# Differential attention's stage: two conv tiles on TensorE from shifted copies, and the rotary swap by ScalarE

## The reference

```
q, k, v, u = split(h @ w_in)                       # 512, 512, 512, 1024 columns
q, k = partial_rope(q), partial_rope(k)            # first 16 of each 64 dims: t1*cos - t2*sin, t2*cos + t1*sin
a = softmax(q1 k1) v - lam * softmax(q2 k2) v      # 4 heads, two 64-wide halves each, causal
a = rmsnorm(a)
c = u[:, :512] * sigmoid(u[:, 512:])
c = causal_depthwise_conv(c, w[31, 512]) + b       # 31 taps per channel
c = silu(layernorm(c))
y = concat(a, c) @ w_out
```

## Time and profile before

| | |
|---|---|
| median of three runs | 2302.03 us (2301.68 to 2302.09) |
| span of the profiled execution, first to last instruction | 2299.9 us |
| that execution's own time outside the span | not printed; median less span is 2.1 us |
| mean granted TensorE clock | 0.999 |
| TensorE busy | 2275.5 us, 99% |
| VectorE, ScalarE, GpSimd busy | 1272.2, 654.6, 1570.5 us |
| DMA | 200.17 MB, mean 87 GB/s |

### The profile page before, as it was taken

The page is one execution under the profiler, slowest core; times in us unless marked ns, Lnnn a source line. Parts: engine busy times, 40 slices in busy tenths (PEclk is TensorE's granted clock), DMA queues, the critical chain, the costliest instruction groups (busy, mean ns, idle before and its releaser), DMA issues.

```text
span 2299.9 us, 27958 instructions
## 1 busy us (share of the span) xinstructions
PE 2275.5 (99%) x10600; PEld 1863.7 (81%) x10600; DVE 1272.2 (55%) x1828; ACT 654.6 (28%) x1213; POOL 1570.5 (68%) x1532
## 2 busy tenths in 40 slices
PE   8999999999999999999999999999999999999998
PEld 6888888888887788888788888888668788888887
DVE  7774745335345777166545364459875345626354
ACT  3443432101013455154311011142344233202113
POOL 8666568777776455545597777678327938878784
PEclk9999999999999999999999999999999999999999
DMA  4222232333332111212243333333113413333332
GB/s 169 82 74 86 70 92 92 105 96 97 96 97 92 51 39 49 74 34 60 73 129 100 97 114 101 93 97 105 56 37 92 124 56 92 96 98 96 99 94 76
DMA packets 112727, 200.17 MB, mean 87 GB/s; under 512 B 12497, under 2 KB 21201, under 8 KB 112593
## 3 DMA queue, kind: packets, MB, share of 16 engines
q1 hardware_dynamic: 109424, 194.72, 27.2%
q10 hardware_dynamic: 3168, 3.67, 0.5%
HBM read 196.24 MB, written 2.10 MB: 86 GB/s over the span
## 4 chain that ended last, share of the span: by engine, by line
PE 93%; DVE 4%; POOL 1%; ACT 1%; issue 0%; DMA 0%; SPq 0%; DVEq 0%; POOLq 0%; ACTq 0%
PE bank L479 27%; PE bank L481 27%; PE bank L480 27%; DVE bank L1996 1%; DVE h L1988 1%; PE bank L949 1%; PE bank L1075 1%; PE bank L528 1%; POOL wL L2857 1%; PE bank L918 1%; PE bank L919 1%; PE bank L920 1%; PE bank L598 1%; DVE aL L1996 1%; PE bank L663 1%; PE bank L926 1%
## 5 line engine op out<-in xcount | busy, mean ns | idle before, releaser
L2857 POOL TENSOR_TENSOR wL<-raw,wH 128x512 fp32r<-128x512 f32 (+2 forms) x732 | 1006.2, 1375 | 61.1
L2855 POOL TENSOR_SCALAR wH<-raw 128x512 fp32r<-128x512 f32 (+2 forms) x732 | 528.6, 722 | 553.5 <-PE bank L481 477.9
L479 PE MATMUL bank<-aH,wH 128*128 128x512 f32 (+2 forms) x1392 | 548.1, 394 | 8.6 <-DVE aL L1996 7.6
L481 PE MATMUL bank<-aH,wL 128*128 128x512 f32 (+2 forms) x1392 | 539.7, 388 | 0.0
L480 PE MATMUL bank<-aL,wH 128*128 128x512 f32 (+2 forms) x1392 | 539.6, 388 | 0.0
L479 PE MATMUL bank<-uH,wH 128*128 128x512 f32 (+1 forms) x1010 | 384.1, 380 | 0.0
L480 PE MATMUL bank<-uL,wH 128*128 128x512 f32 (+1 forms) x1010 | 382.4, 379 | 0.0
L481 PE MATMUL bank<-uH,wL 128*128 128x512 f32 (+1 forms) x1010 | 382.4, 379 | 0.0
L479 PEld LDWEIGHTS bank<-aH,wH 128*128 128x128 f32 (+1 forms) x1392 | 261.8, 188 | 64.7 <-POOL wL L2857 6.6
L480 PEld LDWEIGHTS bank<-aL,wH 128*128 128x128 f32 (+1 forms) x1392 | 261.8, 188 | 55.5 <-issue 3.2
L481 PEld LDWEIGHTS bank<-aH,wL 128*128 128x128 f32 (+1 forms) x1392 | 261.7, 188 | 54.3
(11 more groups left out here) (330 smaller groups left out, 3194.1 us busy)
## 6 DMA issues: line engine op xcount, KB each, us to landing
raw<-in_ws SPq DMA_DIRECT2D x698, 256.0 KB, 2.5
raw<-in_ws SPq DMA_DIRECT2D x24, 192.0 KB, 2.3
h<-in_xT SPq DMA_DIRECT2D x8, 256.0 KB, 6.0
E<-in_memT ACTq DMA_DIRECT2D x16, 128.0 KB, 2.6
raw<-in_ws SPq DMA_DIRECT2D x10, 128.0 KB, 2.1
tmp<-in_pT ACTq DMA_DIRECT2D x4, 256.0 KB, 2.9
out<-c_F SPq DMA_DIRECT2D x2, 512.0 KB, 2.9
out<-c_F SPq DMA_DIRECT2D x2, 384.0 KB, 2.9
```

What stands on the lines that cost most here:

```text
L479: P.e.matmul(o, lH, rH, start=start, stop=False, skip_group_check=skip)
L481: return P.e.matmul(o, lL, rH, start=False, stop=stop, skip_group_check=skip)
L2855: G.e.tensor_scalar(H, x, 1.0, 0.0, MUL, ADD).then_inc(*G.did("wH", n))
L2857: G.e.tensor_tensor(L, x, H.bitcast(F32), SUB).then_inc(*G.did("w", n))
```

## The change

Tiles 2 and 3 of the convolution are TensorE's, tiles 0 and 1 VectorE's. For each of the two, and for each group i of 32 channels, ScalarE's queue issues four DMAs that copy the 32 rows of the gated input into `d_xr[t][i]`, each time one column further, so that one 128-row operand holds four taps of 32 channels. GpSimd builds the weights `d_tw[t]` (128x1024) from a 32-wide identity and the taps (`spread`), among the gate's weight pieces. `conv_rounds` then issues 8 rounds of four matmuls per tile, each 128 rows by 32 columns of weights at its own column position, into 32 partitions of the tile's bank. They go in groups of 16 matmuls. The columns of q and k are ordered anew in the weight pieces (`rotary_spans`), so that the rotary swap exchanges whole groups of 32 partitions; ScalarE does it with four copies of 32 partitions from the bank, and the permutation matmul goes. VectorE's multiply by cos still waits for ScalarE's `rt`. The memory keys move ahead: tile 4 into head 0's part, 5 and 6 into head 1's, 7 into `d_scores(3)`. `xvalues(0)` is opened (its two banks taken) before head 3's transposes, with half of its steps there.

```diff
 def plan():
+            if layer and 4 <= o < 4 + len(BY_PE):
+                spread[len(out)] = o - 4
             tile8("w_ple_gate", layer, 128 * o)
...
+        if h == 3:
+            tile8("w_ckv_2", 0, 128 * 5)
+        add("w_in_2", 0, k8, rotary_spans(128 * h))
+        add("w_in_2", 0, k8, rotary_spans(512 + 128 * h))
+        if h > 1:
+            tile8("w_ckv_2", 0, 128 * (2 * h))
+    tile8("w_ckv_2", 0, 128 * 7)
...
-BY_PE = 3
+BY_PE, BY_DVE = (2, 3), (0, 1)
...
+            def conv_rounds(t, r0, r1):
+                if r0 == 0:
+                    taps[t] = take("ctap", t)
+                    P.wait_ge(G, "tw", t)
+                    P.wait_ge(xr_in[t], 3, 3)
+                for r in range(r0, r1):
+                    for i in range(4):
+                        c = slice(32 * i, 32 * i + 32)
+                        j = P.e.matmul(taps[t].ap[c, :], d_tw[t][:, 128 * r + 32 * i:128 * r + 32 * i + 32],
+                                       d_xr[t][i][:, 4 * r:4 * r + 512], start=r == 0, stop=r == 7, skip_group_check=True,
+                                       tile_position=(0, 32 * i))
+                if r1 == 8:
+                    j.then_inc(*P.did("ctap", t))
+                    give(taps[t], V, "conv", BY_PE[t])
...
             rotary_in(0)
             rotary_in(1)
-            rotate(0)
-            rotate(1)
-            conv_taps(0, 8)
-            d_scores(0, {1: lambda: conv_taps(8, 12), 2: lambda: rotary_in(2)})
+            conv_rounds(0, 0, 4)
+            d_scores(0, {1: lambda: conv_rounds(0, 4, 8), 2: lambda: rotary_in(2)})
             rotary_in(3)
-            rotate(2)
-            rotate(3)
-            conv_taps(12, 16)
+            conv_rounds(1, 0, 4)
             for hd in range(2):
                 d_turned(hd)
-                d_scores(hd + 1, {1: lambda: conv_taps(16 + 8 * hd, 20 + 8 * hd), 2: lambda: rotary_in(2 * hd + 4)})
+                d_scores(hd + 1, {1: lambda: memory_key(4, 1) if hd else conv_rounds(1, 4, 8), 2: lambda: rotary_in(2 * hd + 4)})
                 rotary_in(2 * hd + 5)
-                rotate(2 * hd + 4)
                 d_values(hd)
-                rotate(2 * hd + 5, second=True)
-                conv_taps(20 + 8 * hd, 23 + 8 * hd)
+                memory_key(4 + 2 * hd, 0)
                 stat_end("dn", hd, tiles=1, tail=False)
-                if hd == 0:
-                    conv_taps(23, 24)
             d_turned(2)
...
-            d_scores(3, {1: lambda: memory_keys(4)})
-            memory_keys(6)
+            d_scores(3, {1: lambda: memory_key(6, 1)})
+            d_values(2)
             b = take("stat", "ln")
...
-            d_values(2)
+            values_opened = xvalues_open(0)
+            xvalues_steps(values_opened, range(4))
             d_turned(3)
-            stat_end("dn", 2, tiles=1, tail=False)
-            xvalues(0)
+            stat_end("dn", 2, tiles=1, tail=False, nth=1)
+            xvalues_steps(values_opened, range(4, 8))
             d_values(3)
...
+            def replicate(t):
+                A.wait_ge(V, "glu", BY_PE[t])
+                A.wait_ge(V, "pad")
+                for i in range(4):
+                    for j in range(4):
+                        A.e.dma_start(d_xr[t][i][32 * j:32 * j + 32, :],
+                                      d_cp[32 * i:32 * i + 32, BY_PE[t], j + 1:j + 541]).then_inc(*xr_in[t].did(i, j))
...
-                do(tmp[j % 2][:, :], bk("rt", j)[:, :], ACT.Copy).then_inc(*A.did("rt", j))
+                for q in range(4):
+                    i = do(tmp[j % 2][quarter_rows(q ^ 1), :], bk("rt", j)[quarter_rows(q), :], ACT.Copy)
+                i.then_inc(*A.did("rt", j))
...
-                V.wait_ge(P, "rts", j)
-                stt(t, bk("rts", j)[:, :], s, Sn[:, :], MUL, MUL).then_inc(*V.did("rts", j))
+                V.wait_ge(A, "rt", j)
+                stt(t, t, s, Sn[:, :], MUL, MUL).then_inc(*V.did("rts", j))
...
+            def convolved(t):
+                V.wait_ge(P, "ctap", t)
+                ts(d_acc[:, BY_PE[t], :], bk("ctap", t)[:, :], vv("cv_dw_b_2", BY_PE[t]), None, ADD, None).then_inc(
+                    *V.did("conv", BY_PE[t]))
...
+            def spread(t):
+                G.wait_ge(P, "down done", 1, 3)
+                G.wait_ge(cs_in)
+                G.wait_ge(vs_in)
+                G.e.tensor_tensor(d_tw[t].rearrange("p (g c) -> p g c", c=32), cc("eye32").unsqueeze(1).to_broadcast([128, 32, 32]),
+                                  vv("cv_tap", 32 * t, 32 * t + 32).unsqueeze(2).to_broadcast([128, 32, 32]), MUL).then_inc(
+                    *G.did("tw", t))
```

More of the change, by code:

```diff
@@ L35, in pieces, with rotary_spans @@
     return [(ks[i:i + n], spans) for i in range(0, len(ks), n)]
+def rotary_spans(c0):
+    return tuple((c0 + 64 * i + c, n) for i in range(2) for c, n in ((0, 8), (16, 24), (8, 8), (40, 24)))
 def plan():
-    out, behind = [], {}
+    out, behind, spread = [], {}, {}
     k8 = tuple(range(8))
@@ L172, in plan @@
         down("w_down_2", 0, ks, True)
-    return out, behind, divided
+    return out, behind, divided, spread
 VECS = [
@@ L446, in pe, with take @@
             at = 0
-            def take(*event, second=False):
-                b = banks.pop(1 if second else 0)
+            def take(*event, nth=0):
+                b = banks.pop(nth)
                 if b.freed:
@@ L1034, in rotary_in @@
             def rotary_in(j):
[L1035 to L1039, removed]
-                P.e.matmul(b.ap[:, :], cc("perm_d"), tmp[j % 2][:, :], start=True, stop=True).then_inc(*P.did("rts", j))
-                give(b, V, "rts", j)
+                linear(("rt", j), (V, "rL", j), "w_in_2", 0, 0, aH, aL, n1_ready,
+                       spans=rotary_spans((512 if j % 2 else 0) + 128 * (j // 2)))
             def d_scores(hd, between={}):
@@ L1066, in pe @@
             taps = {}
-            def conv_taps(k0, k1):
-                if k0 == 0:
-                    taps["bank"] = take("ctap")
-                    P.wait_ge(V, "glu", BY_PE)
-                for k in range(k0, k1):
-                    P.wait_ge(A, "dg", k)
-                    P.e.matmul(taps["bank"].ap[:, :], d_dg[k % 8], d_cp[:, BY_PE, 2 + k:514 + k], start=k == 0, stop=k == 30,
-                               skip_group_check=True).then_inc(*P.did("ctap", k))
-                if k1 == 31:
-                    P.also("ctap")
-                    give(taps["bank"], V, "conv", BY_PE)
+            def conv_rounds(t, r0, r1):
[12 more added lines that the diff above has]
+                    give(taps[t], V, "conv", BY_PE[t])
             def d_turned(hd):
                 for kt in range(4):
-                    b = take("dT", hd, kt, second=hd == 2 and kt == 3)
+                    b = take("dT", hd, kt, nth=1 if hd == 2 and kt == 3 else 0)
                     for n in range(kt, 4):
@@ L1814, in convolved @@
                 do(d_acc[:, i, :], bk_acc(i), ACT.Copy).then_inc(*A.did("conv", i))
-            diagonals(0, 8)
+            for t in range(len(BY_PE)):
+                replicate(t)
             convolved(0)
@@ L1832, in act @@
             convolved(1)
-            diagonals(8, 12)
-            d_scores(0, {2: lambda: (diagonals(12, 16), rotary_in(2))})
+            d_scores(0, {2: lambda: rotary_in(2)})
             rotary_in(3)
@@ L1842, in act @@
                     d_turned(0)
-                d_scores(hd + 1, {2: lambda: (convolved(2) if hd else None, diagonals(20 + 8 * hd, 28 + 8 * hd), rotary_in(2 * hd + 4))})
+                d_scores(hd + 1, {2: lambda: rotary_in(2 * hd + 4)})
+                if hd:
+                    memory_keys(4)
                 rotary_in(2 * hd + 5)
@@ L2514, in taps @@
             def taps():
-                for i in range(3):
+                for i in BY_DVE:
                     y = bk_acc(i)
```

124 lines of the change are left out of this document (76 added, 48 removed), and 2 rows, old and new, of the table VECS.

## The result

The changed kernel takes **2319.96 us** (median of four runs, 2319.86 to 2321.05); the kernel before took 2301.86 us beside it (four runs, 2301.55 to 2302.09). The ratio is 1.0082, with an interval of 1.0070 to 1.0093: 18.1 us slower. The direction was forecast, the size was not: 2309.5 us, with a range that ended at 2314.

What follows compares the result with a forecast made beforehand. TensorE, 99% busy, was taken to bound the kernel through its issued work and waits. Terms -33.5 + 27.5 + 1.2 + 7.9 + 2.0 + 2.4 = +7.5 us on 2302.0 gave 2309.5 us, own range 2304 to 2314.

Steps and rivals of the forecast that it cites:

- At nothing: Changes priced at no time: fewer VectorE taps, ScalarE's diagonals gone, its 32 DMA issues, the copies' traffic, reordered weight columns.
- The convolution, two streams: 27.5 us.: TensorE's 64 column-tile matmuls: never more than two stream at once, one new each 0.43 us, adding 27.5 us.
- rival (a): Convolution on TensorE: four matmuls stream at once, 13.7 us instead of 27.5, kernel at 2299.1 us; chance 0.25.
- The bank of `xkL 6`: 7.4 us.: At the opening of `xvalues`: TensorE idles 7.4 us until VectorE frees the second bank (7.9 with the earlier `stat ln` wait).
- The clock: 2.0 us.: After the 7.4 us idle at `xvalues`: TensorE runs at half rate for a while, costing 2.0 us (bounds 0 and 3).
- The rotary chain, 5.5 us, is covered: From `rotary_in(1)` to k's low part: about 5.5 us, covered by 6.9 us of convolution; with four streams TensorE waits 2.1.
- Piece 486: 2.4 us late.: GpSimd's weight pieces: building two tap weights takes 5.2 us and makes piece 486 2.4 us late (bounds 0 and 4).
- Banks and heads, +1.2 us: Heads 0 to 2: TensorE's waits for banks, low parts and transposes total 3.3 us against 2.1 before, so +1.2.

Runs made afterwards that it cites:

- before_copies: The kernel before the change, with only the 32 copy issues added on ScalarE's queue at the change's place: 2314.43 us against 2301.25 (1.0058).
- copies_later: The changed kernel with ScalarE's 32 copy issues put behind `convolved(0)` instead of ahead of it: 2307.91 us (1.0029).
- copies_sync: The changed kernel with the 32 copies issued by SyncE between weight loads, none by ScalarE: 2306.82 us (1.0024).
- tile_by_tile: `both` with seven rounds of tile 0 ahead of head 0's scores, issued column tile by column tile instead of round by round: 2315.62 us (1.0062).
- spread_late: `both` with seven rounds of tile 0 ahead of head 0's scores, and GpSimd's tap weights built before pieces 505 and 507: 2294.76 us (0.9971).
- both: The changed kernel with SyncE issuing the 32 copies and `xvalues_open` skipping the bank of `xkL 6`: 2301.04 us against 2301.52 (0.9996).

## Why the prediction was wrong

- **The step that failed** is the sentence under "At nothing": ScalarE's "32 DMA issues come while it has no other work". At that place they cost 12 to 13 us (`before_copies` +13.2, `copies_later` -12.0, `copies_sync` -13.1). ScalarE had one small copy behind them, `convolved(0)`, and VectorE stood still until it came. I asked whether ScalarE was busy and when the data would land, and not who waits for the instruction behind the issues; nor did I price an issue: 0.64 us, 20.5 us for 32.
- **"The convolution, two streams: 27.5 us."** It is 13.7, rival (a)'s price. My argument was that starts keep program order and each fp32 matmul has two records. `tile_by_tile` shows that starts keep order only within a column tile; the rows of the changed kernel show four at one time.
- **"The bank of `xkL 6`: 7.4 us."** Right: 7.2 in the trace. Taking it away gave 6.0 us.
- **"The clock: 2.0 us."** Right in kind, too small: one fall was forecast, three came, about 7.5 us; the one behind `x_kL` cost 1.6. I had tied it to an idle time of 7 us; it came behind 2.0 us of wait and behind three waits under 0.8 us too. My reading of the start was weaker than I wrote: its rows give the pitch of 0.44 us, but a granted clock of 1.00 beside it. Behind the wait for `x_kL` the same matmuls start 0.43 us apart at a granted 0.50.
- **"The rotary chain, 5.5 us, is covered"**, and with four streams TensorE waits 2.1 us: with the issues away it waits 2.9. The four copies take 2.39 us where I had 2.2.
- **"Piece 486: 2.4 us late."** 1.0 in the trace; the mechanism was right (`spread_late`). What was off is the price of a tap weight: 1.92 us each, not 2.6, so 3.8 us for both instead of 5.2; with that the working gives the 1.0.
- **Banks and heads, +1.2 us**: measured +5.0. All waits of this part but those of 15.7, 7.2 and 1.0 us make 7.1 us, in place of the 2.1 of before. I take it that with four streams TensorE comes earlier everywhere; no run isolates this.

With four streams and the issues priced, the sum would have been 2309.5 - 13.8 + 3.4 + 13 = 2312. By the account above, the other 8 us are the clock (5.5 more than forecast), waits (1.0) and the 1.6 that are not placed; this is rough, since the 13 hold some of the clock already. **That the direction came out right is luck**: a term 13.8 us too high and one of 13 us left out nearly cancel. Without the error on the issues the right price of the column tiles gives rival (a)'s 2299.1, a faster kernel. (The prediction states two ranges, from 2304 and from 2294; both end at 2314.) Rival (a), "what the change is for", was right about the array and wrong about the time: the gain of 19.8 us on TensorE went into waits and the clock.

## What to carry to other kernels

A DMA issue is an instruction of the engine that issues it: count it at its own price, and look at what stands behind it in that program and who waits for that, before asking when the data lands. When TensorE gets less work between two dependencies, move what is left of it ahead of the wait; the rounds moved ahead here were worth more than their length (5.2 us of cover gave 8.7), because the clock stayed up more often. A bank queue that is popped in order hands out waits: walk it again after every reordering.

## Not expected of the hardware

- Four fp32 matmuls on four 32-column tiles run at once, each with two records: 16 matmuls in 3.4 us, where a single one takes 0.86 us.
- The column tiles do not keep a common order of starts: with all of one tile's matmuls first, the next tile started beside the last four records of the one before it (`tile_by_tile`, 1665.09 us).
- A DMA issue of 32 partitions x 2160 bytes holds ScalarE's or SyncE's queue for 0.60 us (0.64 from start to start on ScalarE; four in 2.41 us on SyncE).
- The clock fell behind a wait of 3.0 us with full-width matmuls (0.69 granted in that stretch) as with column tiles (0.83), also behind one of 2.0 us (0.68), and in the one profiled execution not behind one of 1.2 (1.00). Executions of the same program differ in it: eleven of `both` have mean granted clocks from 0.996 to 0.999.
- GpSimd's product of two broadcast operands, 128x1024, takes 1.92 us.
